# First weight part and h brought by quarters in turn on one queue, and fewer unread products ahead of the first stage

## The reference, cut to what matters

```
h = h + 0.5 * swiglu(rms_norm(h, g), w_gate, w_up, w_down)    # stage "f1"
h = h + mixer(rms_norm(h, g2), ...)                           # stage "mix"
h = h + 0.5 * swiglu(rms_norm(h, g3), ...)                    # stage "f2"
```

## Time and profile before

| | us |
|---|---|
| median of 3 runs | 1899.73 |
| lowest and highest | 1899.44, 1900.01 |
| the profiled execution | 1899.96 |
| its span in the profile | 1897.8 |
| TensorE busy in it | 1884.5 |
| VectorE, ScalarE, GpSimd busy | 1340.7, 967.5, 161.5 |

### The profile page before, as it was taken

One profiled execution on the slowest core, in us unless ns is written; L12 is line 12 of the kernel. 1 busy time (PEld: TensorE's weight loads), 2 busy tenths in 40 slices (PEclk: granted clock), 3 DMA queues, 4 the chain that ended last, 5 costly groups with the idle time before them and its releaser, 6 DMA issues.

```text
span 1897.8 us, 26159 instructions
## 1 busy us (share of the span) xinstructions
PE 1884.5 (99%) x10937; PEld 1639.1 (86%) x10940; DVE 1340.7 (71%) x1485; ACT 967.5 (51%) x1216; POOL 161.5 (9%) x158
## 2 busy tenths in 40 slices
PE   9999999999999999999999999999999999999998
PEld 7888879888888888898888888888888888888887
DVE  7877687787687777868776555569765654568764
ACT  5444656544444446665434665455444665455442
POOL 0000522100000006121000200000000110000000
PEclk9999999999999999999999999999999999999999
DMA  7554543455555555334554443445545343445452
GB/s 289 205 185 177 189 153 104 150 200 184 187 196 186 189 182 178 134 112 178 192 190 167 165 171 133 164 169 189 188 173 187 136 174 135 158 178 180 186 176 112
DMA packets 47491, 327.28 MB, mean 172 GB/s; under 512 B 5520, under 2 KB 5520, under 8 KB 11536
## 3 DMA queue, kind: packets, MB, share of 16 engines
q1 hardware_dynamic: 46512, 323.25, 47.0%
q10 hardware_dynamic: 864, 2.38, 0.3%
HBM read 324.56 MB, written 1.05 MB: 172 GB/s over the span
## 4 chain that ended last, share of the span: by engine, by line
PE 97%; DVE 1%; ACT 1%; issue 0%; DMA 0%; POOL 0%; DVEq 0%; POOLq 0%; ACTq 0%
PE ps L537 34%; PE ps L544 18%; PE ps L525 10%; PE ps L527 10%; PE ps L526 10%; PE ps L865 2%; PE ps L531 1%; PE ps L831 1%; PE ps L820 1%; PE ps L822 1%; PE ps L821 1%; PE ps L854 1%; PE ps L582 1%; PE ps L532 1%; PE ps L741 1%
## 5 line engine op out<-in xcount | busy, mean ns | idle before, releaser
L331 ACT CAST w_hi<-raw 128x2048 fp32r<-128x2048 f32 (+4 forms) x314 | 580.1, 1849 | 574.0 <-PE ps L527 193.7
L338 DVE TENSOR_TENSOR w_lo<-raw,w_hi 128x2048 fp32r<-128x2048 f32 (+4 forms) x314 | 700.1, 2231 | 237.8 <-ACT w_hi L331 235.1
L537 PE MATMUL ps<-x_hl,w_hi 128*128 128x512 f32 x1968 | 459.3, 390 | 0.0
L537 PEld LDWEIGHTS ps<-x_hl,w_hi 128*128 128x128 f32 x1968 | 365.2, 188 | 73.2
L525 PE MATMUL ps<-w_hi,x_hl 128*128 128x512 f32 (+3 forms) x672 | 262.5, 391 | 0.0
L527 PE MATMUL ps<-w_hi,x_hl 128*128 128x512 f32 (+3 forms) x672 | 254.3, 378 | 0.0
L526 PE MATMUL ps<-w_lo,x_hl 128*128 128x512 f32 (+3 forms) x672 | 253.6, 377 | 0.0
L544 PEld LDWEIGHTS ps<-x_hl,w_lo 128*128 128x128 f32 x1968 | 243.6, 192 | 5.5 <-DVE w_lo L338 1.4
L544 PE MATMUL ps<-x_hl,w_lo 128*128 128x256 f32 x1968 | 246.8, 283 | 0.8 <-DVE w_lo L338 0.8
L1816 DVE TENSOR_REDUCE ffn_tmp<-ps 128x512 f32<-128x1024 f32 x132 | 161.2, 1223 | 100.3 <-PE ps L544 50.2
L537 PE MATMUL ps<-hid_hl,w_hi 128*128 128x512 f32 x836 | 196.4, 390 | 0.0
(11 more groups left out here) (288 smaller groups left out, 2204.3 us busy)
## 6 DMA issues: line engine op xcount, KB each, us to landing
raw<-in_parts SPq DMA_DIRECT2D x278, 1024.0 KB, 4.8
raw<-in_parts SPq DMA_DIRECT2D x20, 768.0 KB, 4.2
raw<-in_parts SPq DMA_DIRECT2D x4, 928.0 KB, 4.5
raw<-in_parts SPq DMA_DIRECT2D x4, 864.0 KB, 4.4
raw<-in_parts SPq DMA_DIRECT2D x6, 512.0 KB, 3.7
raw<-in_parts SPq DMA_DIRECT2D x4, 576.0 KB, 3.6
const<-in_const ACTq DMA_DIRECT2D x1, 1093.0 KB, 5.1
h<-in_x_t SPq DMA_DIRECT2D x1, 1024.0 KB, 7.6
```

The lines of the kernel that those rows point to most:

```text
L331: nc.scalar.copy(w_hi[:, i % RING, 0:n_of(i)], raw[:, i % RING, 0:n_of(i)]).then_inc(high_ready, 1)
L338: nc.vector.tensor_tensor(w_lo[:, s, 0:n], raw[:, s, 0:n], w_hi[:, s, 0:n].bitcast(F32), ALU.subtract).then_inc(low_ready, 1)
L537: m = nc.tensor.matmul(ps[:, bank, :], w_h(c), hl(c).rearrange("p x n -> p (x n)"), start=start and c == 0, stop=stop and c == kc - 1, ski ...
```

## The change

The first part and h come in four quarters each, on the same queue, in turn (quarter of part 0, then the two chunks of h that it is multiplied with), all ahead of part 1. Each quarter has a semaphore of its own. ScalarE and VectorE work in the same turn: piece q of part 0, then chunks 2q and 2q + 1 of h. Eight transfers of 256 KB with rows of 2 KB replace two of 1 MB with rows of 8 KB. The unread products behind the first cast are four in place of ten. As part 0 has its own semaphores, the count that slot 0 waits for is one lower from part 3 on.

```
@@ -268,7 +268,7 @@
-        x_in = sem("x_in")
+        x_in, first_in = [sem(f"x_in{q}") for q in range(4)], [sem(f"first_in{q}") for q in range(4)]
@@ -311,7 +311,7 @@
-            act.wait_ge(raw_in[i], 16)
+            act.wait_ge(raw_in[1] if i else first_in[q], 16)
@@ -325,7 +325,7 @@
-            act.wait_ge(raw_in[i % RING], 16 * (i // RING + 1))
+            act.wait_ge(raw_in[i % RING], 16 * (i // RING + (i % RING > 0)))
@@ -503,9 +503,11 @@
         def _(sp):
-            for i in range(NP_):
-                if i == 1:
-                    sp.dma_start(h[:, :, :], w["x_t"]).then_inc(x_in, 16)
+            for q in range(4):
+                a, n = piece(0, q)
+                sp.dma_start(raw[:, 0, a:a + n], w["parts"][0, :, a:a + n]).then_inc(first_in[q], 16)
+                sp.dma_start(h[:, 2 * q:2 * q + 2, :], w["x_t"][:, 2 * q:2 * q + 2, :]).then_inc(x_in[q], 16)
+            for i in range(1, NP_):
                 if i >= RING:
@@ -1210,7 +1212,7 @@
             pe.wait_ge(first_hi, 1)
-            warm_up(10, 7)
+            warm_up(4, 7)
@@ -1659,9 +1661,9 @@
             for q in range(4):
                 piece_hi(act, 0, q)
-            act.wait_ge(x_in, 16)
-            for c in range(KC):
-                next_x(0, c, wait=False)
+                act.wait_ge(x_in[q], 16)
+                for c in (2 * q, 2 * q + 1):
+                    next_x(0, c, wait=False)
@@ -2298,9 +2300,9 @@
             for q in range(4):
                 piece_lo(dve, 0, q)
-            dve.wait_ge(x_in, 16)
-            for c in range(KC):
-                next_x_lo(0, c)
+                dve.wait_ge(x_in[q], 16)
+                for c in (2 * q, 2 * q + 1):
+                    next_x_lo(0, c)
```

## The result

| | before, us | changed kernel, us |
|---|---|---|
| median | 1899.72 (20 runs) | **1902.41** (20 runs) |
| lowest and highest | 1899.07, 1900.33 | 1901.61, 1903.61 |
| span of the profiled execution | 1897.8 | 1900.3 |

The ratio is 1.0015, 95% interval 1.0009 to 1.0021. The forecast was 1898.4, shorter by 1.4, with a range of 1897.0 to 1900.0; the kernel became longer by 2.7. It is the side of rival C.

What follows compares the result with a forecast made beforehand. TensorE, busy 1884.5 of 1897.8 us, was taken as the bound; the spreading of the root, 1.4 us earlier, carried to the end: 1899.96 - 1.4 = 1898.6, 1898.3 from the median, given as 1898.4, range 1897.0 to 1900.0.

Steps and rivals of the forecast that it cites:

- rival C: Loads at the head: gaps between quarters delay part 1 and the root, gain gone at landing 13.1; chance 0.1.
- The quarters: Loads of part 0 and h: 2 KB packets at 0.085 us each make part 1 land 0.47 later, at 11.7.
- The bound given for this price: Quarter loads: at most 0.310 us for each of 64 packets, 14.4 us more; at the other end nothing.
- Rival D: At the root: TensorE need not wait, or part 1 lands at 11.25; gain 1.8 to 2.4 us, chance 0.12.
- The gains no longer hold ScalarE until 6.5: ScalarE's start at the head: the gains land at 4.7 in place of 6.5, first cast at 4.72.
- rival B: ScalarE's start: gains still land at 6.5, so no earlier start; 1898.6, chance 0.53 together with the forecast.
- Part 1's wait of TensorE of 1.85: TensorE after part 0's products: from 12.25 it waits 1.85 us for part 1's low piece.
- The root ends last: Before the spreading: TensorE comes at 27.5 and waits for GpSimd's root until 28.6; spreading 1.36 us earlier.
- Rival A: TensorE's clock falls after the 1.85 us wait: 1.7 us lost, gain only 0.75, 1899.0; chance 0.25.
- Four in place of ten cost nothing: Unread products at the head: dropping six (1.3 us) costs nothing, being under TensorE's wait of 1.85 for part 1.

Runs made afterwards that it cites:

- e3: The kernel before, still with two transfers of 1 MB, but read from copies laid out by contiguous quarters, so in 2 KB packets; 1899.44 us, ratio 0.9999.
- e4: The changed kernel with the quarters of part 0 and h each in one piece in HBM instead of rows 8 KB apart; 1898.74 us, ratio 0.9995.
- e12: The kernel before with VectorE's mean of the squares moved ahead of part 4's low half, nothing else; 1899.66 us, ratio 0.9999.
- e8: The contiguous version (e4) with ten unread products behind the first cast in place of four; 1898.36 us, ratio 0.9993.
- e11: The kernel before with four unread products behind the first cast in place of ten, loads untouched; 1901.66 us, ratio 1.0010.
- e6: The changed kernel with halves in place of quarters: four transfers of 512 KB, rows of 4 KB at a pitch of 8 KB; 1899.48 us, ratio 1.0000.

## Why the prediction was wrong

**The step that failed** is the price in "The quarters": "I take the 2 KB row, which has the same size, though it goes out and not in". The price of 0.085 us for a packet was right for the size (e3: 0.45 us for both megabytes, 0.47 forecast), and wrong for where the rows lie. Part 0 and h are read by quarters of rows that are 8 KB apart, two such streams in turn; the row that I took the price from said nothing on the pitch, and I did not list it as unknown. In place of 0.47 us the quarters cost 15.8 - 11.25 = 4.55. The bound given for this price, up to 14.4 us more, held it, and the range did not take in that bound: I let the evidence against gaps between transfers count against every other reason for a late part 1.

**A slip in rival C** made that range look safer than it was. By its own rule a lateness of 2.4 us (gaps of 0.4) gives 1898.4 + 2.4 = 1900.8, outside the range, and not the 1899.4 that stands there; the 1912.3 behind it follows the rule.

**The rest of the chain held.** Rival C's rule, that a late landing of part 1 falls on the root "us for us", with the gain gone at 13.1, gives -1.36 + (15.8 - 11.7) = +2.7 for the changed kernel: measured +2.69, both in the time and at the spreading. Its mechanism was another: the queue had no gaps, its engines were busy and slow. e4 shows the other side: eight transfers of rows side by side cost nothing beyond their packets.

**Point by point.** Rival D is out: at the root in e4 the weight loads waited 0.85 (1.1 forecast) and the products 0.64. The gains no longer hold ScalarE until 6.5: right (5.41 in the changed kernel, 3.78 in e4), rival B is out. Part 1's wait of TensorE of 1.85: 1.6 in e4, 1.9 in the changed kernel, where another of 2.4 stands before it. The root ends last: right in both, with 1.2 us of slack before (e12: no gain from an earlier root). The gain without the pitch: 1.36 at the spreading, forecast 1.36; in the medians 1.1 (1899.80 to 1898.74), with an interval of the ratio that takes in 1. That the first agrees so well is in part luck: it compares with one execution of before, 0.24 over its median, and in e12, with the same head, the spreading started at 29.32. Rival A, the clock: out, in the changed kernel and in e4 at 1.00. "Four in place of ten cost nothing": right here (e8), for the reason given, a wait for part 1 longer than they are. It would not have been right without the quarters (e11).

**What stays open.** Why a pitch of 8 KB is slow and 10 and 12 are not was not shown; the profile names no part of HBM. The 1.3 us that went with other tensors at the same pitch are unexplained. The Trainium skill (DMA: Bandwidth & Descriptors, "Latency and other measured facts") reports slow copies between HBM tensors at row pitches of 2 MB and more, advises a few KB of padding or a contiguous layout, and names channels of HBM as an unverified reason. The cure agrees with the runs here (2 and 4 KB of padding, or one piece). The pitch does not: here 8 KB was slow. Why the clock fell in some executions and not in others is open too, as the last section lists.

## What to carry to other kernels

A transfer cut from wider rows can be priced by its pitch too, and not by its bytes and packets alone (here at 8 KB, with two such streams): where a piece is wanted early, lay it out in HBM as one piece, or pad the rows, and look at the GB/s under a full DMA share. Unread products were free while a wait behind them covered them (e8), and dear to leave out where the engine idled instead (e11). And a first read product that starts 4.8 us earlier (5.87 in e4, 10.66 before) brought 1.1 in the median, since two other waits, for part 1 and for the root, stood behind it: find the last wait before counting the first.

## What the runs showed that was not expected

- Cutting two loads of 1 MB at the 8 KB pitch by columns took the rate at 2 to 5 us from 335 to 171 GB/s with the engines' busy share at 0.83; contiguous quarters kept 321.
- The same pieces at pitches of 10 and 12 KB landed within 0.05 us of the contiguous ones; one stream at 8 KB cost 0.55 us, two 2.7 to 4.05.
- Transfers to 32 partitions moved 223 GB/s, half the rate of whole ones.
- Idle time of 2.1 us on either side of four unread products was followed by the 1.2 GHz level; 2.4 and 1.9 us among read products were not. Nor did the length of the idle time tell elsewhere: the clock fell after 0.8 and 1.5 us (e6) and stayed up through 1.6 and 0.8 (e3) and 1.5 and 0.8 (e12).
- GpSimd's root beside a VectorE subtraction took 2.62 us in place of 0.71, in both runs in which the two met.
